# Hybrid attention and recurrence block: small levels read row by row, rounded means, value copies and additions moved

## The reference

```
u = rmsnorm(x);  proj = u @ w_in          # q,k,v of 8 attention heads; q, two forget gates, values, gate of 4 recurrent heads
y_na = neighbourhood attention over a 16 x 64 grid, windows 8 x 16, relative bias, softmax
y_hg = for each of 4 heads, forward and backward:
          S_t = diag(f_t) S_{t-1} + (1 - f_t) v_t^T;   o_t = S_t^T q_t
       o = rmsnorm(o_fwd + o_bwd over its 128 channels) * gnorm * silu(g)
h = x + concat(y_na, y_hg) @ w_out
h = h + square(relu(rmsnorm(h) @ w_up)) @ w_down
```

## Time and profile before

| | |
|---|---|
| median of 3 runs | 1300.78 us (1299.91 to 1301.66) |
| the profiled execution: its time | 1302.38 us |
| its span, first to last instruction | 1300.5 us |
| TensorE busy | 1280.9 us, 98% |
| VectorE, ScalarE, POOL busy | 64%, 45%, 36% |
| attention steps (2) | about 99 to 294 us of the span |
| recurrent heads (3) | 294 to 575 us |
| output projection (4) | 575 to 667 us |
| MLP (5) | from there to the end |

### The profile page before, as it was taken

The page is one execution under the profiler, slowest core; times in us unless marked ns, Lnnn a source line. Parts: engine busy times, 40 slices in busy tenths (PEclk is TensorE's granted clock), DMA queues, the critical chain, the costliest instruction groups (busy, mean ns, idle before and its releaser), DMA issues.

```text
span 1300.5 us, 17647 instructions
## 1 busy us (share of the span) xinstructions
PE 1280.9 (98%) x6432; PEld 1077.8 (83%) x6432; DVE 838.1 (64%) x1260; ACT 583.5 (45%) x1049; POOL 474.1 (36%) x259
## 2 busy tenths in 40 slices
PE   7999999999999999999999999999999999999998
PEld 6878887998888888888888788888888888888887
DVE  3637666541758685966477545445455888888885
ACT  6346766445444453350255554454453433433341
POOL 3341212115040504055134544544543544544452
PEclk9999999999999999999999999999999999999999
DMA  7341333222010101142311644545559463533433
GB/s 247 130 126 49 100 88 87 73 66 82 1 50 1 50 17 49 66 147 97 130 65 48 227 139 155 166 128 159 165 199 372 140 241 97 191 133 98 162 94 133
DMA packets 134469, 154.92 MB, mean 119 GB/s; under 512 B 11376, under 2 KB 89584, under 8 KB 134384
## 3 DMA queue, kind: packets, MB, share of 16 engines
q1 hardware_dynamic: 131216, 147.04, 35.0%
q10 hardware_dynamic: 3168, 6.75, 1.4%
HBM read 109.72 MB, written 44.04 MB: 118 GB/s over the span
## 4 chain that ended last, share of the span: by engine, by line
PE 92%; DVE 4%; ACT 2%; issue 1%; DMA 1%; POOL 0%; ACTq 0%; SPq 0%; DVEq 0%
PE bank L2307 8%; PE bank L2310 8%; PE bank L2311 8%; PE bank L2276 7%; PE bank L2279 7%; PE bank L2280 7%; PE bank L2020 6%; PE bank L2024 6%; PE bank L2023 6%; PE bank L2106 5%; PE bank L2233 2%; PE bank L2237 2%; PE bank L2236 2%; PE bank L1918 1%; PE bank L2007 1%
## 5 line engine op out<-in xcount | busy, mean ns | idle before, releaser
L865 POOL TENSOR_TENSOR w_hi<-stage,one_col 128x1024 fp32r<-128x1024 f32 x32 | 61.8, 1931 | 417.3 <-DVE scores L1584 178.1
L923 POOL TENSOR_TENSOR a_split<-a_raw,a_split 128x1024 fp32r<-128x1024 f32 x56 | 148.0, 2660 | 166.1 <-ACT a_split L1196 166.1
L2276 PE MATMUL bank<-set,w_hi 128*128 128x512 f32 x448 | 177.9, 397 | 0.3 <-DVE s L1814 0.2
L2279 PE MATMUL bank<-set,w_hi 128*128 128x512 f32 x448 | 176.2, 393 | 0.0
L2280 PE MATMUL bank<-set,w_lo 128*128 128x512 f32 x448 | 176.1, 393 | 0.0
L2307 PE MATMUL bank<-w_hi,a_split 128*128 128x512 f32 x448 | 174.7, 390 | 0.2
L2310 PE MATMUL bank<-w_lo,a_split 128*128 128x512 f32 x448 | 174.5, 389 | 0.0
L2311 PE MATMUL bank<-w_hi,a_split 128*128 128x512 f32 x448 | 174.4, 389 | 0.0
L2020 PE MATMUL bank<-uT_hi,w_hi 128*128 128x512 f32 x384 | 160.2, 417 | 0.0
L2024 PE MATMUL bank<-uT_hi,w_lo 128*128 128x512 f32 x384 | 150.5, 392 | 0.0
L2023 PE MATMUL bank<-uT_lo,w_hi 128*128 128x512 f32 x384 | 149.8, 390 | 0.0
(11 more groups left out here) (222 smaller groups left out, 2746.9 us busy)
## 6 DMA issues: line engine op xcount, KB each, us to landing
a_raw<-a_dram SPq DMA_DIRECT2D x56, 512.0 KB, 3.7
a_dram<-abuf SPq DMA_DIRECT2D x111, 256.0 KB, 2.1
stage<-in_w_in SPq DMA_DIRECT2D x29, 512.0 KB, 4.1
raw<-in_w_down SPq DMA_DIRECT2D x10, 1024.0 KB, 8.1
stage<-in_w_up SPq DMA_DIRECT2D x16, 512.0 KB, 5.5
raw_b<-in_w_up SPq DMA_DIRECT2D x16, 512.0 KB, 5.7
x_tok<-in_x SPq DMA_DIRECT2D x8, 512.0 KB, 8.8
v_dram<-vs ACTq DMA_DIRECT2D x16, 256.0 KB, 2.3
```

The costliest lines, as they stand in the source:

```text
L923: pool.tensor_tensor(split_of(m, 1), a_raw[:, m % 4, :, :], split_of(m, 0).bitcast(F32), ALU.subtract).then_inc(b_lo, 1)
L2276: first = pe.matmul(dst, w[0], u[0], start=k == 0 and p in (1, 5, 6, 7), stop=False, skip_group_check=True)
L2279: pe.matmul(dst, w[0], u[1], start=False, stop=False, skip_group_check=True)
```

## The change

Four parts.

1. For n = 0 and 1 (levels 1 and 2), `chunk_queries` no longer exchanges block and direction: the moving columns come in the order direction, block, element. So that each result stands where it stood, the PSUM destination is viewed the same way (`chunk_place`): for n = 0 every second float32 is written, for n = 1 two of every four.
2. The mean over channels uses rounded passes. ScalarE rounds `tmp` into `o_sq_hi` (two more operations of 128 x 512 for each head), VectorE subtracts to `o_sq_lo` (two more of 128 x 512, both inputs in SBUF), and TensorE makes four fp32r matmuls in the place of two float32 ones. `o_sq_hi` lies over `k_tok` and `o_sq_lo` over `state`, which are dead then. The means of heads 0 to 2 move from behind level 0 to behind level 1, ScalarE's roots from piece 0 to piece 2, VectorE's result from piece 2 to piece 3. Of head 3 the mean moves from behind product 0 to behind product 1, and ScalarE runs the last gate unit before the squares.
3. In attention step 9 ScalarE copies the first value unit right after the second exponential; each copy waits only for the scores of its own row group. On TensorE `share(2)` of step 9 (the second unit) moves behind `times_values(9, 2)`.
4. VectorE adds the first two products to `resid` before the result of head 3. Since `resid` tiles 3 to 7 lie over the new tiles, SP loads tiles 0 to 2 as before and the others one weight tile later, after the means.

```diff
         def chunk_queries(n, c):
             blocks = CHUNK // (2 * HALVES[n])
-            return query_halves(n)[:, :, blocks * c:blocks * c + blocks, :].rearrange("p d b x -> p b d x")
+            v = query_halves(n)[:, :, blocks * c:blocks * c + blocks, :]
+            return v if n < 2 else v.rearrange("p d b x -> p b d x")
+        def chunk_place(n, t):
+            return t.rearrange("p (b d x) -> p d b x", d=2, x=HALVES[n]) if n < 2 else t
...
                 if n == N_IN + RING + 1:
                     sp.wait_ge(o_done, 2 * HG_HEADS)
-                    for t in range(TT):
-                        sp.dma_start(resid[:, t, :], x_v[:, t, :]).then_inc(resid_load[t], 16)
+                    load_resid(range(3))
+                if n == N_IN + RING + 2:
+                    sp.wait_ge(o_mean, 2 * HG_HEADS)
+                    load_resid(range(3, TT))
...
                 elif kind == "hv":
-                    if (what, part) == (0, 0):
-                        act.wait_ge(score_done, NG * NB * (PAIRS - 1))
+                    if what == 0 and part < NG:
+                        act.wait_ge(score_done, NG * (NB * (PAIRS - 1) - 1) + part + 1)
...
+            def round_squares(h):
+                for part in range(2):
+                    act.wait_ge(o_sq, 2 * h + part + 1)
+                    act.wait_ge(upd_done, 4 * (h + 1))
+                    act.activation(o_sq_hi[:, part, :], tmp[:, part, :], ACT.Copy).then_inc(o_sq_rounded, 1)
...
                     if s + 2 < STEPS:
                         score_exp(s + 2, g)
+                    if s == 9 and g == 1:
+                        unit(values[0])
                 if s == 9:
-                    for n in values:
-                        unit(n)
+                    unit(values[1])
...
                         take_diagonal(h)
-                        if h:
-                            head_roots(h - 1)
+                    if i == 2 and h:
+                        head_roots(h - 1)
...
+                        if h == HG_HEADS - 1:
+                            for n in HEAD_UNITS[h][i]:
+                                unit(n)
                         head_squares(h)
+                        round_squares(h)
...
+            def squares_lo(h, part):
+                dve.wait_ge(o_sq_rounded, 2 * h + part + 1)
+                dve.wait_ge(o_done, 2 * (h + 1))
+                dve.tensor_tensor(o_sq_lo[:, part, :], tmp[:, part, :], o_sq_hi[:, part, :].bitcast(F32),
+                                  ALU.subtract).then_inc(o_sq_rest, 1)
...
                         first_queries(h)
+                        if h:
+                            squares_lo(h - 1, 0)
+                            squares_lo(h - 1, 1)
...
-                    if i == 2 and h:
+                    if i == 3 and h:
                         head_result(h - 1)
...
-            head_result(HG_HEADS - 1)
             for part in range(2):
-                gated_part(HG_HEADS - 1, part)
+                squares_lo(HG_HEADS - 1, part)
...
+            dve.wait_ge(resid_load[0], 16)
+            for n in range(2):
+                dve.wait_ge(down_done, n + 1)
+                add_bank(n, 0)
+            head_result(HG_HEADS - 1)
+            for part in range(2):
+                gated_part(HG_HEADS - 1, part)
+            for n in range(2, 3 * 2 * TT):
...
             def head_means(h):
+                pe.wait_ge(mean_ready, 1)
                 for part in range(2):
-                    pe.wait_ge(o_sq, 2 * h + part + 1)
-                    pe.matmul(bank[4 + part][:, :], all_mean, tmp[:, part, :], start=True, stop=True).then_inc(o_mean, 1)
+                    pe.wait_ge(o_sq_rest, 2 * h + part + 1)
+                    pe.matmul(bank[4 + part][:, :], mean_r[:, :], o_sq_hi[:, part, :], start=True, stop=False)
+                    pe.matmul(bank[4 + part][:, :], mean_r[:, :], o_sq_lo[:, part, :], start=False, stop=True).then_inc(o_mean, 1)
...
-                share(2)
+                if s != 9:
+                    share(2)
                 if s >= 0:
                     times_values(s, 2)
+                if s == 9:
+                    share(2)
```

More of the change, by code:

```diff
@@ L686, in load_v_weights, with load_resid @@
                 sp.dma_start(dst, w_in_v[:, a:b, C_V:C_V + HALF]).then_inc(v_w_load[i], 16)
+            def load_resid(tiles):
+                for t in tiles:
+                    sp.dma_start(resid[:, t, :], x_v[:, t, :]).then_inc(resid_load[t], 16)
             load_x(0)
@@ L1276, in _ @@
             hgrn_may_start(act)
+            act.activation(mean_r[:, :], all_mean, ACT.Copy).then_inc(mean_ready, 1)
             for n in FIRST_HEAD:
@@ L1304, in _ @@
                             unit(n)
+                        if h == HG_HEADS - 1:
+                            for n in HEAD_UNITS[h][i]:
+                                unit(n)
                         head_squares(h)
+                        round_squares(h)
                     last = [n for n in HEAD_UNITS[h][i] if i < 9 or UNITS[n][0] != "hq"]
-            for n in last:
-                unit(n)
             head_roots(HG_HEADS - 1)
@@ L1751, in up_sum @@
                     dve.tensor_tensor(here, up_operand(j, 2), here, ALU.subtract).then_inc(x_sum, 1)
-            for n in range(3 * 2 * TT):
+            dve.wait_ge(resid_load[0], 16)
[6 more added lines that the diff above has]
+            for n in range(2, 3 * 2 * TT):
                 i = n % (2 * TT)
@@ L2104, in level @@
                         else:
-                            k, q = chunk(near(i - 1), c), chunk_queries(i - 1, c)
-                        ins = pe.matmul(bank[2 + cg][:, P * (c % 4):P * (c % 4) + P], k, q, start=True, stop=True)
+                            k, q, dst = chunk(near(i - 1), c), chunk_queries(i - 1, c), chunk_place(i - 1, dst)
+                        ins = pe.matmul(dst, k, q, start=True, stop=True)
                     ins.then_inc(lev_done, 1)
@@ L2209, in _ @@
                         level(h, i)
-                        if i == 0 and h:
+                        if i == 1 and h:
                             head_means(h - 1)
```

9 lines of the change are left out of this document (8 added, 1 removed).

## The result

The changed kernel takes 1293.07 us (median of 4 executions, 1291.82 to 1293.81) where the kernel before takes 1300.96 (1299.91 to 1301.66) beside it: ratio 0.9936, 95% interval 0.9924 to 0.9948. Two executions of the whole record, one of the kernel before (1417 us, granted clock 0.85) and one of `read_four` (2142 us, 0.56), were slow from end to end, and the ratios leave them out. The profiled execution has a span of 1292.0 us, TensorE is busy for 99% of it.

What follows compares the result with a forecast made beforehand. TensorE, busy 98% of the span, was taken to bound the kernel. Gains of 4.0 + 1.4 + 4.3 - 1.2 = 8.5 us from a median of 1300.8 gave 1292.3 us, range 1288.5 to 1297.5.

Steps and rivals of the forecast that it cites:

- Part 1: Levels 1 and 2, four times: both would cost what contiguous level 0 does, 4.0 us gained.
- The bounds for the slow write: Level 1's stepped PSUM writes: half pace loses 3.0 us in all (chance 0.14), a third of the pace loses 10.0 on level 1.
- the number of jumps between directions: Levels 1 and 2: the excess shrinks with these jumps, 64 pairs a chunk 0.84 us, 32 pairs 0.15; the new order jumps once.
- The rule for PSUM: Writes of levels 1 and 2: PSUM has 8-byte lines, so any non-contiguous access slows matmuls significantly; level 1 would pay, level 2 not.
- Part 2 in the heads: Rounded means of heads 1 to 3: 0.82 us gained each if nothing waits, but -0.2 in head 2; 1.4 in all.
- The collision of head 2: VectorE's subtractions take turns with POOL's splits: TensorE pauses about 0.7 us at the mean, 0.3 more in level 2.
- Part 3: Steps 9 and 10: 2.27 us of wait, 0.5 of pause and 1.6 of clock gained; 4.3 taken, ends 2.3 and 4.5.
- The 1.6 us of clock: Behind TensorE's wait for the value copy: without that wait the clock stays up, gaining 1.6 of 1.7 us lost.
- Output projection: Its start: subtractions collide with two POOL splits, TensorE pauses about 2.4 us behind product 1; 1.2 us lost.
- The rival without a collision: Output projection: VectorE's subtraction gets in before POOL or POOL's splits come later; 2.7 us better, 1289.6; chance 0.17.
- The clock behind the new pause: Output projection: the clock falls at the new pause of some 2.4 us; 1.7 us more, 1294.0; chance 0.20.
- the slower case: Level 1: stepped PSUM writes at a third of the pace, 0.32 us a record, 1305.7; over 2.6 us slower from 0.27; chance 0.04.

Runs made afterwards that it cites:

- read_four: Changed kernel, but level 1 reads every fourth float32 (16-byte steps) and writes PSUM without steps: 1299.90 us, ratio 0.9989 to the kernel before.
- stride_four: Changed kernel, but level 1 both reads and writes PSUM in steps of 16 bytes: 1299.93 us, ratio 0.9990 to the kernel before.
- the halves: Kernel before with one half of part 3 each: ScalarE's early copy alone, 1298.98 us; TensorE's moved second value unit alone, 1300.83 us.
- split_held: Changed kernel, but POOL starts the last split of the input weights only after both subtractions of head 3: 1290.71 us, ratio 0.9918 to the kernel before.
- psum_squares: Changed kernel, but ScalarE writes the squares to PSUM, so VectorE's subtraction has one input there: 1290.04 us, ratio 0.9914 to the kernel before.
- part24_only: Changed kernel without parts 1 and 3, so the kernel before with parts 2 and 4: 1300.45 us, ratio 0.9995 to the kernel before.

## Why the prediction was right, point by point

The forecast was 1292.3 us with 1288.5 to 1297.5, and 1293.07 came out. It is nearer than its terms deserve: one term of 1.6 us did not come, and 1.2 us came that it did not have.

- **Part 1: right, cause only half.** 4.0 was counted, 3.6 measured, of which the writes cost at most 0.1 a head. The bounds for the slow write did not come true, at any place. But the reason given for taking 4.0, that the number of jumps between directions is what costs, is wrong: `stride_four` and `read_four` have one jump and cost 1.8 us a level. The prediction's own numbers spoke against it: level 2 has half the jumps of level 1 and under a fifth of the excess (0.15 against 0.84). Reads in one direction cost nothing extra as long as they take two elements of each 16 bytes, and since the changed order does that, both views gave the same number here. Why the alternating order of level 1 lies in between, at 0.164, neither view explains. The rule for PSUM did not come true on level 1; the prediction exempted level 2 from it as filling whole lines, though the rule as quoted takes in every access that isn't contiguous, and it did not come true there either.
- **Part 2 in the heads: right.** 0.82 was counted for a mean, 0.79 measured. The collision of head 2 was foreseen with its splits, the pause 0.7 and 0.3 more in level 2, measured 0.38 and 0.28; so 0.1 was left where -0.2 was expected.
- **Part 3: mechanism right, one term wrong.** The 2.27 of the wait and half a microsecond of the moved unit came (2.14 and 0.55 in the halves, 2.65 together). The 1.6 us of clock did not come as a term of the comparison: the profiled execution had a fall that at least 24 of 67 executions of the kernel before did not have. The warning was in the prediction's own numbers, as the profiled execution was 1.6 us over the median, just what the stretch at the lower level cost. Having taken the gain from the median, it should have left the 1.6 out or counted a share of it.
- **Output projection: right.** Its reading of the earlier trace rows took a TENSOR_SCALAR for an operation with two inputs in SBUF, which changes nothing for the subtractions. -1.2 counted, -1.36 measured, with the two splits, the first subtraction behind the first of them, and the pause of 1.98 where 2.4 was named. The pause of 0.5 before product 4 went as counted: 0.54 is gained there in the trace. The rival without a collision is what `split_held` and `psum_squares` then built: its 2.7 us are the 2.67 of the traces.
- **The clock behind the new pause** was given 0.20. It is in neither profile of the changed kernel, and eight of nine executions show a clock of 1.000, so it did not happen here as a rule; `part24_only`, with the same pause, shows that it can.
- **Not foreseen:** 1.2 us at the end of the program. It nearly made up for the clock term, 8.5 counted against 7.9 in the traces. Without this luck the forecast, 0.8 us too low as it is, would have been 2 us too low.
- **A sum:** by the prediction's own terms the slower case begins at 0.28 us a record, not 0.27, since (2.6 + 0.6 + 4.5) / 64 is 0.12 more than 0.164. No chance hangs on it.
- **Head 3:** VectorE did not become the bound, no wait of level 5 shows.

## What to carry to other kernels

When a subtraction is added on VectorE beside a busy POOL, keep one of its inputs in PSUM, or hold POOL back where it has time: here the first was worth 3.0 us and the second, at one place, 2.4. That is more than the 1.6 that the rounded means gained in the two heads where nothing collided. Let the moving operand of a float32 matmul take at least two elements of each 16 bytes that it passes, without alternating between two places, and put the stepping into the PSUM write; for matmuls of another type nothing here was measured. Before counting a low clock as part of a kernel's time, compare the profiled execution with the median: what only one execution shows is not to be gained. And when a part alone gives the expected time, compare its terms too: in `part24_only` they were other ones.

## What the hardware showed that was not expected

- A pause of TensorE of 2.0 to 2.1 us was followed by 3.4 us at the lower clock level in 2 of 10 profiles and by nothing in the other 8, once each way with the same kernel. One kernel lost clock in all eleven executions, the changed one, with one of its two pauses, in one of nine.
- A record of a float32 matmul of 128 columns (two records each) takes 0.113 us with reads in steps of 8 bytes, 0.227 in steps of 16 bytes, and 0.164 when they alternate between two places; the writes to PSUM in steps of 8 or 16 bytes cost 0.04 us a level or less. The 0.227 is the same at a granted clock of 0.56, where other records slow from 0.11 to 0.20.
- The time behind the last matmul goes with where instruction loading falls: with one packet of 8 KB among the last stores it was 4.2 to 5.0 us in six profiles, without it 3.8 in seven. The cause was not tested.
